# A block of weights fetched later in the prologue, and its two parts made between halves of h

## The chip, the cores and the metric

One core of a Trainium2 chip. The metric is device time in microseconds, the median of several runs. The engines are TensorE (PE), VectorE (DVE), ScalarE (ACT), GpSimd (POOL) and SyncE (SP), which issues every DMA of this kernel.

## What is computed

One step of a hybrid decoder layer over a prompt of 2048 rows and 8 sample rows, width 1024, in float32. Cut to what bears on this case:

```
mod = c @ w_ada + b_ada
shift, scale, gate = split(mod, 3)
h = rms_norm(x, norm_g) * (1 + scale) + shift
proj = h @ w_in      # q, k, v, za for window attention; q, f, i, z for the recurrence
... window attention with sinks; HGRN2 recurrence; both gated ...
y = sigmoid(h @ w_merge + b_merge) gates (ya @ w_proj_a) and (yb @ w_proj_b)
out = x + gate * (y @ w_out)
```

## The kernel before, in words

**Products in three parts.** Each operand of a dense product is split into a high part (float32r, made by ScalarE with a copy) and a low part (the rest, made by GpSimd with a subtraction). TensorE sums high x high, high x low and low x high (`dense`, lines 719 to 755).

**Tiles.** The prompt goes in four iterations of 512 rows. Each iteration is a list of units; a unit is one TensorE result in bank D0 or D1, run in two halves of the contraction (`hf_` 0 and 1), with side tasks between. The first four units of iteration 0 are B tiles: 128 rows of h against the three blocks q3, k and v. A block is 1024 x 128 weights, 512 KB. k and v are fetched in pieces of 128 numbers (512 bytes), q3 in pieces of 64, into one of three raw buffers (`block_dmas`, line 466). Block numbers 0, 1 and 2 are q3, k and v.

**The prologue.** mod needs all of `w_ada`'s first 2048 columns. They come in two halves, each as eight DMAs of 512 KB in pieces of 2 KB: `ada_load(k, 0)` (lines 523, 524), then `ada_load(k, 1)` (lines 633, 634). The last DMA of a half goes to the tile th_t. TensorE multiplies a half as pairs of tiles land (`ada_half`, line 678), turns the result rows into columns (`turn_rows`, line 688), and VectorE makes shift and scale from them (`modulation`, line 1239). The first half serves contraction slices 0 to 3 of h, the second slices 4 to 7. `modulate_half(t, q)` (line 1229) makes half q of tile t of h from the turned x, ScalarE its high part (`h_high_half`, line 982; semaphore `h_hi`), GpSimd its low part (lines 1701 to 1704; semaphore `h_lo`).

**Order on each engine, written out by hand.** SyncE: first-half modulation weights, blocks q3, k, v (lines 631, 632), second-half modulation weights, then small constants, then the gate weights. ScalarE: the high parts of the three blocks (lines 999, 1000), h halves (0,0) and (1,0), after the eighth modulation step (`p_mod` 8) the copy of a result bank (line 1003), h halves (0,1), (1,1), and those of tiles 2 and 3. GpSimd: the low parts of the three blocks (lines 1699, 1700), four subtractions each (`split_lo`, line 1677), then the eight low halves of h. TensorE: the first half of modulation, turns of x tiles 0 and 1, the second half of modulation, `turn_rows(1)`, dense half 0 of unit 0, the eight turns of x tile 2, dense half 1 of unit 0, the turns of x tile 3, and so on.

**What TensorE waits for.** Ahead of the first half of a unit, the low parts of all its blocks and with unit 0 the first low half of h:

```
s.wait_ge("w_lo", it * NB + blocks[-1] + 1)
...
if it == 0 and u < NT:
    s.wait_ge("h_lo", (1, 3, 2, 4, 5, 6, 7, 8)[2 * u + hf_])
```

For unit 0 the first of these is `w_lo` >= 3: the low parts of q3, k and v. Semaphores count up in the order in which the parts are made. SyncE issues block 3 only after the first side task that reads raw block 0 (line 808).

Of the kernel before, what the change touches and what calls it, by code (L numbers as in the profile page):

```python
# [50 lines left out]
NSLOT, NRAW = 6, 3  # L51
# [39 lines left out]
SPOT, HOLDER, ATTACH, BURST_AT = [], [], {}, {}  # L91
# [165 lines left out]
def h_tiles(it, t):  # L257

    return 8 + 4 * it + t + 1 if it >= 0 else 2 * t + 2
# [52 lines left out]
def build(nc, A, O):  # L312

    ctx = ExitStack()
    with ctx:
# [93 lines left out]
        def f32(ap):  # L409
            return ap.bitcast(F32)  # L410
# [55 lines left out]
        def block_dmas(n):  # L466

            kind, j = BLOCKS[n % NB]
            dst = w_raw[:, n % NRAW]
            if kind in ("q", "za"):  # L470
                c = (C_QA if kind == "q" else C_ZA) + DH * j
                return [(dst[:, :, DH * g:DH * g + DH],
                         w_in[:, c + 256 * g:c + 256 * g + DH].rearrange("(k p) c -> p k c", p=P))
                        for g in range(G)]
            if kind == "pa":
                cs = slice(P * j, P * j + P)
                return [(dst[DH * g:DH * g + DH, 0:4, :],
                         w_pa[256 * g:256 * g + 256, cs].rearrange("(m p) c -> p m c", p=DH))
                        for g in range(G)] + [(dst[:, 4:8, :],
                                               w_pb[:, cs].rearrange("(h p) c -> p h c", p=P))]  # L480
            base = {"f": C_FB, "qb": C_QB, "k": C_KA, "v": C_VA, "ib": C_IB, "zb": C_ZB}
            src, c0 = ((w_in, base[kind] + P * j) if kind in base else
                       (w_out, P * j) if kind == "out" else (w_merge, P * j + (D if kind == "gb" else 0)))
            return [(dst, src[:, c0:c0 + P].rearrange("(k p) c -> p k c", p=P))]
# [16 lines left out]
        def _(sp):  # L501
            s = Eng(sp, "none", S)

            def load(dst, src, name, **kw):
                s.done(sp.dma_start(dst, src, **kw), name, by=16)  # L505
# [6 lines left out]
            def ada_load(k, h):  # L512
                load(ada[k].rearrange("p (s h n) -> p s h n", s=2, h=2)[:, :, h],
                     A["w_ada"][0, P * k:P * k + P, 0:2 * D].rearrange("p (s h n) -> p s h n", s=2, h=2)[:, :, h], f"ada{KT * h + k}")
# [11 lines left out]
            def weights(n):  # L526
                if n >= NRAW:
                    s.wait_ge("w_lo", n - NRAW + 1)
                    if n - NRAW in bursts:
                        s.wait_ge(*bursts[n - NRAW])  # L530
                for dst, src in block_dmas(n):
                    load(dst, src, f"w_in{n % NRAW}")
# [95 lines left out]
                    s.freed(1, "sOT", 1)  # L628
                    load(O[1][:, 0, :], rowsS[:, 0:D], "fin")

            for n in range(NRAW):
                weights(n)
            for k in range(KT):
                ada_load(k, 1)
            load(ones[:, :], A["c_ones"], "p_load2")
            load(eye32[:, :], A["c_eye32"], "p_load2")
            load(lm_in, A["c_lmask"], "p_load2")
# [318 lines left out]
        def _(act):  # L956
# [3 lines left out]
            def split_hi(n):  # L960
                s.wait_ge(f"w_in{n % NRAW}", came[n])
                if HOLDER[n] >= 0:
                    s.unit_full(*divmod(HOLDER[n], NU))
                s.done(fn(w_hi[:, SLOT[n % NB]], w_raw[:, n % NRAW], ACT.Copy), "w_hi")  # L964
# [17 lines left out]
            def h_high_half(t, q):  # L982
                s.freed(-1, "xT", t) if q else s.wait_ge("hm", t + 1)
                k = slice(4 * q, 4 * q + 4)
                s.done(fn(h_hi[:, k, P * t:P * t + P], hf[t % 2][:, k], ACT.Copy), "h_hi")
# [10 lines left out]
                scale_x(-1, t, x_p[t])  # L996
            s.wait_ge("p_lb", 1)
            s.done(fn(lbt[:, 1:3, :], lbt[:, 1:3, :], ACT.Exp), "p_exp0")
            for n in ATTACH[-1]:
                split_hi(n)  # L1000
            h_high_half(0, 0), h_high_half(1, 0)
            s.wait_ge("p_mod", 8)
            s.done(fn(mod_rows[:, 512:1024], pb["D1"][:, :], ACT.Copy), "p_rows")
            h_high_half(0, 1), h_high_half(1, 1)
            for t in (2, 3):
                h_high_half(t, 0), h_high_half(t, 1)
# [665 lines left out]
        @blk.gpsimd  # L1672
        def _(pool):
            g_ = nc.gpsimd
            s = Eng(pool, "pool_step", S)

            def split_lo(n):
                s.wait_ge("w_hi", n + 1)
                c = SLOT[n % NB]
                for k in range(0, KT, 2):  # L1680
                    ins = g_.tensor_tensor(w_lo[:, c, k:k + 2], w_raw[:, n % NRAW, k:k + 2], f32(w_hi[:, c, k:k + 2]),  # L1681
                                           ALU.subtract)
                s.done(ins, "w_lo")

            def h_low(it, t):
                s.wait_ge("h_hi", h_tiles(it, t))
                c = slice(P * t, P * t + P)
                for k in range(0, KT, 2):
                    ins = g_.tensor_tensor(h_lo[:, k:k + 2, c], hf[t % 2][:, k:k + 2], f32(h_hi[:, k:k + 2, c]), ALU.subtract)
                s.done(ins, "h_lo")  # L1690

            def low(dst, hi, n):
                s.wait_ge("yh", n + 1)
                src = yf[:, n % 2, :]
                if dst.shape[-1] != TB:
                    src = src.rearrange("p (m n) -> p m n", m=4)
                s.done(g_.tensor_tensor(dst, src, f32(hi), ALU.subtract), "yl", n + 1)

            for n in ATTACH[-1]:
                split_lo(n)  # L1700
            for n, (t, q) in enumerate(((0, 0), (1, 0), (0, 1), (1, 1), (2, 0), (2, 1), (3, 0), (3, 1))):
                s.wait_ge("h_hi", n + 1)
                k, c = slice(4 * q, 4 * q + 4), slice(P * t, P * t + P)
                s.done(g_.tensor_tensor(h_lo[:, k, c], hf[t % 2][:, k], f32(h_hi[:, k, c]), ALU.subtract), "h_lo")
            for it in range(NIT):
                for u in range(NU):
                    for hf_ in (0, 1):
                        if hf_:
                            if UNITS[u] == ("pb", 7):
                                s.wait_ge("y7h", it + 1)  # L1710
                                s.done(g_.tensor_tensor(y_lo[:, 7, 0:P], yf[:, 1, 0:P], f32(y_hi[:, 7, 0:P]), ALU.subtract), "y7l")
                                s.wait_ge("yh", 16 * it + 16)
                                s.done(g_.tensor_tensor(y_lo[:, 7, P:TB], yf[:, 1, P:TB], f32(y_hi[:, 7, P:TB]),
                                                        ALU.subtract), "yl", 16 * it + 16)
                            for n in ATTACH.get(it * NU + u, []):
                                split_lo(n)
                        for task, a, _, key in SIDE.get((it, u, hf_), []):
                            if task == "at0":
                                if it:
                                    s.full(it - 1, "xT", 3)  # L1720
                                    s.freed(it - 1, "xT", 3)
                                else:
                                    s.freed(0, "gb", 0)
                                    s.freed(0, "gS", 0)
                                for c in range(0, 2048, 512):
                                    ins = g_.memset(R1[:, c:c + 512], 0.0)
                                s.done(ins, "at0")
                            elif task == "hh":
                                h_low(it, a)
                            elif task == "PV":  # L1730
                                c = slice(P * a, P * a + P)
                                low(ya_lo[:, :, c], ya_hi[:, :, c], 16 * it + a)
                            elif task == "yT":
                                c = slice(P * a, P * a + P)
                                low(yb_lo[:, :, c], yb_hi[:, :, c], 16 * it + 4 + a)
                            elif task == "vB":
                                s.wait_ge(f"s_st{a}", 16)
                                o = s_st[a].rearrange("p (h n) -> p h n", h=HB)
                                s.done(g_.tensor_tensor(o, o, fS[:, :, a:a + 1].broadcast_to([P, HB, P]), ALU.mult), "s_f")
                        if hf_ and UNITS[u][0] == "pb" and UNITS[u][1] < 7:  # L1740
                            j = UNITS[u][1]
                            low(y_lo[:, j, :], y_hi[:, j, :], 16 * it + 8 + j)
# [56 lines left out]
```

## Time and profile before

| | us |
|---|---|
| median of 3 runs | 1580.97 |
| lowest and highest run | 1580.01, 1585.47 |
| profiled execution | 1582.4 |
| its span in the trace | 1580.4 |

The profile shows one execution, with times in microseconds from the start of the span. "PEclk", or the third figure from the end in a stretch, is the clock that the throttle granted to TensorE as a share of full speed: 1 is 2.4 GHz, 0.5 is 1.2 GHz. The DMA share is the mean busy share of the core's 16 DMA engines; it can read slightly above 1. In brackets behind an instruction stands how long its engine was idle before it, and what released it. L750 and L753 are the dense matmuls, L685 the modulation matmuls, L692 the turns of the result rows, L964 a block's high part, L1681 a block's low part, L985 a high half of h, L1704 a low half of h.

### The profile page before, as it was taken

The numbers are of one execution on the slowest core, as the hardware profiler recorded it, in microseconds if no ns is written. First come the engines' busy times: TensorE is split into PE (matmuls) and PEld (weight loads), VectorE is DVE, ScalarE is ACT, GpSimd is POOL, SyncE is SP. The second block draws the span as 40 slices with busy tenths as digits, with TensorE's granted clock in tenths as the row PEclk, the third lists the DMA queues.
The fourth block names the chain that finished last, engine by engine and source line by source line (L and its number), as shares of the span: only waits on it lengthen the run. The fifth ranks groups of instructions, "written<-read, shape, count | busy, mean of one in ns | idle before, by whom it ended". The sixth has DMA issues, their size and how long they took to land.

```text
span 1580.4 us, 32835 instructions
## 1 busy us (share of the span) xinstructions
PE 1547.7 (98%) x13544; PEld 1257.3 (80%) x13544; DVE 776.6 (49%) x1946; ACT 554.8 (35%) x1131; POOL 824.6 (52%) x1080
## 2 busy tenths in 40 slices
PE   5999999999999999999999999999999999999998
PEld 2787788877888777888778877888888977788886
DVE  3667455233458865432345775722334775623132
ACT  4334323434322541433422352244432353243330
POOL 2435324457674552455756373437777363437671
PEclk9999999999999999999999999999999999999999
DMA  9723212344565331233365331224455331223351
GB/s 316 236 75 95 69 56 68 93 121 120 173 170 130 95 95 52 71 97 118 94 188 135 84 101 53 82 67 120 142 179 145 87 108 55 69 67 93 101 167 62
DMA packets 304972, 175.88 MB, mean 111 GB/s; under 512 B 74158, under 2 KB 290567, under 8 KB 304808
## 3 DMA queue, kind: packets, MB, share of 16 engines
q1 hardware_dynamic: 304824, 173.79, 37.8%
q8 instruction: 107, 1.75, 0.5%
q14 instruction: 41, 0.34, 0.1%
HBM read 159.69 MB, written 11.96 MB: 109 GB/s over the span
## 4 chain that ended last, share of the span: by engine, by line
PE 95%; DVE 2%; SPq 2%; DMA 1%; issue 1%; ACT 0%; DVEq 0%
PE ps_D L753 56%; PE ps_D L750 25%; PE ps_XD L808 2%; SPq L505 2%; PE ps_XA L907 1%; PE ps_XB L885 1%; PE ps_XB L933 1%; PE ps_XA L938 1%; PE ps_XB L932 1%; PE ps_XA L918 1%; DMA th_t<-in_w_ada 1%; PE ps_XA L885 1%; PE ps_XB L918 0%; PE ps_XC L925 0%; PE ps_XC L820 0%
## 5 line engine op out<-in xcount | busy, mean ns | idle before, releaser
L1681 POOL TENSOR_TENSOR w_lo_t<-w_raw,w_hi_t 128x256 fp32r<-128x256 f32 x928 | 678.3, 764 | 628.6 <-ACT w_hi_t L964 628.6
L753 PE MATMUL ps_D<-h_hi_t,w_hi_t 128*128 128x512 f32 x1024 | 412.9, 403 | 0.0
L753 PE MATMUL ps_D<-h_lo_t,w_hi_t 128*128 128x512 f32 x1024 | 399.9, 391 | 0.0
L753 PE MATMUL ps_D<-h_hi_t,w_lo_t 128*128 128x512 f32 x1024 | 399.9, 391 | 0.0
L964 ACT ACTIVATE w_hi_t<-w_raw 128x1024 fp32r<-128x1024 f32 x232 | 240.2, 1051 | 80.5 <-PE ps_D L750 44.7
L753 PEld LDWEIGHTS ps_D<-h_hi_t,w_hi_t 128*128 128x128 f32 x1024 | 192.3, 188 | 49.1 <-issue 12.0
L753 PEld LDWEIGHTS ps_D<-h_hi_t,w_lo_t 128*128 128x128 f32 x1024 | 192.2, 188 | 41.8
L753 PEld LDWEIGHTS ps_D<-h_lo_t,w_hi_t 128*128 128x128 f32 x1024 | 192.6, 188 | 36.1
L750 PE MATMUL ps_D<-w_hi_t,h_hi_t 128*128 128x384 f32 (+1 forms) x384 | 141.0, 367 | 2.2 <-issue 1.5
L750 PE MATMUL ps_D<-w_lo_t,h_hi_t 128*128 128x384 f32 (+1 forms) x384 | 136.3, 355 | 0.0
L750 PE MATMUL ps_D<-w_hi_t,h_lo_t 128*128 128x384 f32 (+1 forms) x384 | 136.0, 354 | 0.0
L750 PE MATMUL ps_D<-w_hi_t,y_hi_t 128*128 128x512 f32 x256 | 101.1, 395 | 0.0
L750 PE MATMUL ps_D<-w_lo_t,y_hi_t 128*128 128x512 f32 x256 | 99.7, 390 | 0.0
L750 PE MATMUL ps_D<-w_hi_t,y_lo_t 128*128 128x512 f32 x256 | 99.7, 390 | 0.0
L1355 DVE SCALAR_TENSOR_TENSOR acc_t<-th_t,ps_D 128x512 f32<-128x512 f32 x24 | 16.5, 688 | 139.3 <-PE ps_D L753 139.3
L1031 ACT ACTIVATE th_t<-ps_D,bm_half 128x512 f32<-128x512 f32 x48 | 33.1, 689 | 142.1 <-PE ps_D L753 142.1
L750 PEld LDWEIGHTS ps_D<-w_hi_t,h_hi_t 128*128 128x128 f32 x384 | 72.4, 189 | 10.0 <-issue 3.6
L1107 ACT ACTIVATE p_or_hf<-p_or_hf,sm 128x160 f32<-128x160 f32 x128 | 53.5, 418 | 72.5 <-DVE sm L1482 68.8
L750 PEld LDWEIGHTS ps_D<-w_hi_t,h_lo_t 128*128 128x128 f32 x384 | 72.5, 189 | 6.1 <-issue 1.4
L750 PEld LDWEIGHTS ps_D<-w_lo_t,h_hi_t 128*128 128x128 f32 x384 | 72.4, 188 | 5.3
L1435 DVE TENSOR_TENSOR qq<-qq,ff 128x1024 f32<-128x1024 f32 x28 | 40.9, 1460 | 70.4 <-PE ps_XB L885 44.8
L1524 DVE SCALAR_TENSOR_TENSOR state<-state,ff,ps_XA 128x128 f32<-128x128 f32 x64 | 18.0, 342 | 112.8 <-PE ps_XA L938 112.8
(391 smaller groups left out, 2375.7 us busy)
## 6 DMA issues: line engine op xcount, KB each, us to landing
w_raw<-in_w_in SPq DMA_DIRECT2D x72, 512.0 KB, 4.0
w_raw<-in_w_merge SPq DMA_DIRECT2D x64, 512.0 KB, 4.0
w_raw<-in_w_in SPq DMA_DIRECT2D x64, 256.0 KB, 4.0
w_raw<-in_w_out SPq DMA_DIRECT2D x32, 512.0 KB, 3.8
x_or_AT<-in_x_prompt SPq DMA_DIRECT2D x20, 512.0 KB, 5.1
w_raw<-in_w_proj_a SPq DMA_DIRECT2D x64, 128.0 KB, 3.0
w_raw<-in_w_proj_b SPq DMA_DIRECT2D x32, 256.0 KB, 3.2
xr<-in_x_prompt SPq DMA_DIRECT2D x16, 512.0 KB, 5.3
```

The costliest lines, as they stand in the source:

```text
L505: s.done(sp.dma_start(dst, src, **kw), name, by=16)
L750: ins = mm(bank[:, 0:P * nb].rearrange("p (n c) -> p n c", c=P), a[:, k, P * j:P * j + P], w[:, s0:s0 + nb, k, :], start=go, stop=end)
L753: ins = mm(bank[:, :], w[:, s0, k0 + k, :], a[:, k, :], start=go, stop=end)
L808: ins = mm(bank[32 * (k % 4):32 * (k % 4) + 32, P * c:P * c + P], hS[:, k, :], raw[:, k, :], start=k < 4, stop=k >= 4)
L885: ins = mm(bank[row:row + left, m * col:m * col + m], kk[:, h, c + 32 * g:c + 32 * g + left], right, start=True, stop=True)
L964: s.done(fn(w_hi[:, SLOT[n % NB]], w_raw[:, n % NRAW], ACT.Copy), "w_hi")
L1031: s.leave(fn(dst, bank[:, :], ACT.Tanh, scale=0.5, bias=bm_half[:, c:c + 1]), it, u)
L1107: fn(p_t[:, m, :], p_t[:, m, :], ACT.Exp, bias=negm[:, m:m + 1], accum_out=rsum[:, m:m + 1])
L1355: leave(stt(acc[:, :], thx("ga", j), 1.0, bank[:, :], ALU.add, ALU.mult), it, u)
L1435: s.done(tt(qr, qr, fl[:, :, :, 0:1].broadcast_to(shape), ALU.mult))
L1524: ins = stt(state[:, h, :], state[:, h, :], ff[:, h, P * a:P * a + 1], bank[:, P * h:P * h + P], ALU.mult, ALU.add)
L1681: ins = g_.tensor_tensor(w_lo[:, c, k:k + 2], w_raw[:, n % NRAW, k:k + 2], f32(w_hi[:, c, k:k + 2]), ALU.subtract)
```

## The change

The v block (number 2) is issued behind the second-half modulation weights. Its high part comes on ScalarE behind the copy of the result bank, its low part on GpSimd between the second and the third low half of h, after GpSimd's wait for the third high half. Nothing else is edited.

```diff
--- before.py
+++ after.py
@@ -628,10 +628,10 @@
                     s.freed(1, "sOT", 1)
                     load(O[1][:, 0, :], rowsS[:, 0:D], "fin")
 
-            for n in range(NRAW):
-                weights(n)
+            weights(0), weights(1)
             for k in range(KT):
                 ada_load(k, 1)
+            weights(2)
             load(ones[:, :], A["c_ones"], "p_load2")
             load(eye32[:, :], A["c_eye32"], "p_load2")
             load(lm_in, A["c_lmask"], "p_load2")
@@ -996,11 +996,11 @@
                 scale_x(-1, t, x_p[t])
             s.wait_ge("p_lb", 1)
             s.done(fn(lbt[:, 1:3, :], lbt[:, 1:3, :], ACT.Exp), "p_exp0")
-            for n in ATTACH[-1]:
-                split_hi(n)
+            split_hi(0), split_hi(1)
             h_high_half(0, 0), h_high_half(1, 0)
             s.wait_ge("p_mod", 8)
             s.done(fn(mod_rows[:, 512:1024], pb["D1"][:, :], ACT.Copy), "p_rows")
+            split_hi(2)
             h_high_half(0, 1), h_high_half(1, 1)
             for t in (2, 3):
                 h_high_half(t, 0), h_high_half(t, 1)
@@ -1696,11 +1696,12 @@
                     src = src.rearrange("p (m n) -> p m n", m=4)
                 s.done(g_.tensor_tensor(dst, src, f32(hi), ALU.subtract), "yl", n + 1)
 
-            for n in ATTACH[-1]:
-                split_lo(n)
+            split_lo(0), split_lo(1)
             for n, (t, q) in enumerate(((0, 0), (1, 0), (0, 1), (1, 1), (2, 0), (2, 1), (3, 0), (3, 1))):
                 s.wait_ge("h_hi", n + 1)
                 k, c = slice(4 * q, 4 * q + 4), slice(P * t, P * t + P)
+                if n == 2:
+                    split_lo(2)
                 s.done(g_.tensor_tensor(h_lo[:, k, c], hf[t % 2][:, k], f32(h_hi[:, k, c]), ALU.subtract), "h_lo")
             for it in range(NIT):
                 for u in range(NU):
```

## Rows read from the trace of the kernel before

**Rows 1.** The page: TensorE's busy time, and the chain that ended last by engine.
```profile
PE 1547.7 (98%) x13544; PEld 1257.3 (80%) x13544; DVE 776.6 (49%) x1946; ACT 554.8 (35%) x1131; POOL 824.6 (52%) x1080
...
PE 95%; DVE 2%; SPq 2%; DMA 1%; issue 1%; ACT 0%; DVEq 0%
```

**Rows 2.** Waits of TensorE, 44 to 200 us (total, times, longest us).
```profile
PE ps_XC L692 <- DVE qq L1292: 0.9, 1, 0.9
PE ps_D L750 <- DVE yf_t L1321: 0.7, 1, 0.7
```

**Rows 3.** Chain of waits, 0 to 80 us (start, length us, what).
```profile
28.95 12.91 DMA th_t<-in_w_ada
...
41.99 1.05 PE ps_D L685 x4
...
44.75 1.95 PE ps_XC L692 x16
46.71 3.21 PE ps_D L750 x12
...
51.38 2.08 PE ps_D L750 x12
```

**Rows 4.** Timeline of TensorE (start, length us, instruction, idle before it).
```profile
32.34 1.03 PE L685 MATMUL ps_D<-qq,cT_or_ab 128*32 128x512 f32 x1 [3.26 <-DMA ff<-in_w_ada]
...
46.56 0.42 PE L750 MATMUL ps_D<-w_hi_t,h_hi_t 128*128 128x384 f32 x1
...
48.11 0.52 PE L750 MATMUL ps_D<-w_hi_t,h_lo_t 128*128 128x384 f32 x1
48.43 0.52 PE L750 MATMUL ps_D<-w_lo_t,h_hi_t 128*128 128x384 f32 x1
...
49.71 1.67 PE L705 MATMUL ps_XA<-ident,s_st_lo 128*128 128x128 f32 x8
51.14 0.42 PE L750 MATMUL ps_D<-w_hi_t,h_hi_t 128*128 128x384 f32 x1
```

**Rows 5.** Timeline of GpSimd, 20 to 90 us.
```profile
25.95 8.25 POOL L1681 TENSOR_TENSOR w_lo_t<-w_raw,w_hi_t 128x256 fp32r<-128x256 f32 x12 [25.51 <-ACT w_hi_t L964]
...
49.42 2.69 POOL L1704 TENSOR_TENSOR h_lo_t<-p_or_hf,h_hi_t 128x512 fp32r<-128x512 f32 x2 [12.77 <-ACT h_hi_t L985]
...
61.74 5.57 POOL L1681 TENSOR_TENSOR w_lo_t<-w_raw,w_hi_t 128x256 fp32r<-128x256 f32 x8 [2.50 <-ACT w_hi_t L964]
...
83.25 3.34 POOL L1681 TENSOR_TENSOR w_lo_t<-w_raw,w_hi_t 128x256 fp32r<-128x256 f32 x4 [3.03 <-ACT w_hi_t L964]
```

**Rows 6.** Timeline of ScalarE, 20 to 60 us.
```profile
26.58 1.06 ACT L964 ACTIVATE w_hi_t<-w_raw 128x1024 fp32r<-128x1024 f32 x1 [0.70 <-DMA w_raw<-in_w_in]
28.68 1.06 ACT L964 ACTIVATE w_hi_t<-w_raw 128x1024 fp32r<-128x1024 f32 x1 [1.04 <-DMA w_raw<-in_w_in]
...
43.94 0.60 ACT L1003 ACTIVATE qq<-ps_D 128x512 f32<-128x512 f32 x1 [10.31 <-PE ps_XD L685]
48.71 0.63 ACT L985 ACTIVATE h_hi_t<-p_or_hf 128x512 fp32r<-128x512 f32 x1 [4.18 <-DVE p_or_hf L1235]
```

**Rows 7.** Stretches: busy us by engine, granted clock, DMA share, GB/s.
```profile
24.00:26.00 2.00, 2.00 (x16) 1.36 (x13) 1.18 (x2) 1.06 (x1) 0.04 (x1) 1.00 1.03 278
26.00:28.00 2.00, 2.00 (x22) 1.81 (x20) 0.11 (x1) 1.06 (x1) 2.00 (x3) 1.00 1.05 268
...
32.00:34.00 2.00, 1.66 (x4) 0.43 (x6) 0.96 (x4) 0.85 (x2) 2.00 (x4) 0.50 1.04 389
...
40.00:42.00 2.00, 0.01 (x2) 0.04 (x3) 0.00 (x0) 0.00 (x0) 0.00 (x0) 1.00 0.64 227
46.00:48.00 2.00, 2.00 (x14) 2.00 (x14) 1.19 (x6) 0.00 (x0) 0.00 (x0) 0.90 1.01 408
48.00:50.00 2.00, 2.00 (x8) 1.90 (x8) 1.96 (x7) 0.63 (x1) 0.58 (x1) 0.50 1.04 416
50.00:52.00 2.00, 2.00 (x13) 2.00 (x12) 1.22 (x5) 0.63 (x1) 1.87 (x2) 0.75 1.04 389
```

## The prediction

> **What bounds the kernel now.** I read the page first, to see which engine sets the time. TensorE is busy for 98% of the span and makes 95% of the chain that ended last [rows 1]. Then the list of TensorE's waits after the prologue: from 44 to 200 us it waits twice, for 0.9 and 0.7 us [rows 2]. The reader is to see that nothing after the prologue has room to take up a delay: what the start of the first dense unit gains or loses should reach the end.
>
> Then the chain of waits over the prologue. The last second-half modulation weights (th_t) are issued at 28.95 and hold the chain for 12.91 us, until TensorE takes them at 41.99. The last matmuls on it follow, the copy to mod_rows, the 16 row turns from 44.75 to 46.70, and at 46.71 the dense matmuls [rows 3]. The one idle time between is the 0.9 us for the copy [rows 2]. So today the first dense half starts when TensorE has done its own work, not when a weight is ready. TensorE's timeline gives 46.56 for its first matmul [rows 4]. The v block is not on that path: its low part is the last third of a GpSimd stretch that ends at 25.95 + 8.25 = 34.20 [rows 5], 12.4 us before that matmul.
>
> **The change part by part.**
>
> **1. The transfer of v leaves the queue ahead of the second modulation half.** SyncE issues one DMA fewer there and one more behind; the work of issuing is the same. The price of v in the queue: ScalarE waits for each block's data and starts on k at 26.58 and on v at 28.68, so v took 2.10 us [rows 6]. In 24 to 28 us the engines moved 278 and 268 GB/s at full share [rows 7]; 512 KB, which is 524,288 bytes, by 270 is 1.94 us. I take 1.9. Lower bound: while modulation weights of the same size moved, the rate was 389 GB/s [rows 7], so 1.35 us. Upper bound: near th_t's landing (40 to 42 us) the engines were busy for a share of only 0.64 [rows 7], so the last piece sits on an engine that lags; if v's pieces cost that engine more by the unused 0.36 of 2 us, v is worth 2.1 + 0.7 = 2.8. Gain 1.9 (1.35 to 2.8).
>
> The Trainium skill (DMA: Bandwidth & Descriptors, Specifications) says that pieces of 512 bytes or more move at line rate. v is fetched in pieces of 128 numbers, 512 bytes, and this trace disagrees: its blocks move at 268 to 278 GB/s where modulation weights get 389. By the page the gain would be 1.35 and the result 0.55 us later than my sum.
>
> **2. ScalarE's high part of v moves behind the copy of the second half's rows.** The copy starts at 43.94 and the next instruction, the high part of h's tile 0, second half, only at 48.71, after 4.18 us idle for VectorE [rows 6]. The 1.06 us of v fit there. v's data: as many bytes lie ahead of it as now lie ahead of th_t, so it lands near 41.9 (where th_t lands now), before ScalarE asks at about 44.54 - 1.9 = 42.6. Cost 0. If that cover were gone, it would need v to land after 45.7.
>
> **3. GpSimd's low part of v moves, and behind a wait.** This decides. In the new code GpSimd first waits for the third high half of h, and only then runs the four subtractions for v. The third high half is ScalarE's at 48.71, with 0.63 us, so it ends at 49.34; GpSimd answers at 49.42 [rows 5]. TensorE's first dense half waits for the low part of all three blocks, v's included. Today that wait was met at 34.2. In the new order it is met when four subtractions after 49.42 are done. Their price: 12 took 8.25 us, so 2.75 for four; the next eight took 5.57, so 2.79 [rows 5]. I take 2.8, with bounds 2.75 and 3.34, the dearest group [rows 5]. With 0.05 for the handover, the first dense matmul comes at 49.42 + 2.80 + 0.05 = 52.27 by today's clock of events, where it now comes at 46.56: 5.7 us later. Both times shift together by the 1.9 of part 1, since the third high half hangs on VectorE's modulation (the releaser of the instruction at 48.71 [rows 6]), and that on th_t.
>
> Who waits behind it: on GpSimd the low parts of h, third and fourth half, come 2.8 us later, at about 52.3 and 53.5 less 1.9. TensorE asks for the third only after the first dense half and eight turns, 4.6 us after its new start (as from 46.56 to 51.14 [rows 4]), about 55. VectorE's tile 2 waits for that third half as well, but also for TensorE's turns, which end later. Cost of both 0; the cover is TensorE's own delay. TensorE holds everything behind its wait, above all the turns of tile 2, which stand behind the dense half in its order and can't fill the gap. All later loads hang on TensorE (the next weight block is issued once the first sample burst is done) and shift with it.
>
> **4. The clock.** TensorE will stand idle from the end of the row turns (46.70 - 1.9 = 44.8) to 50.4, for 5.6 us. Before, it stood idle for 3.26 us ahead of 32.34 [rows 4], and the granted clock then fell to 0.50 (1.2 GHz), where it still was in 32 to 34 us with TensorE busy [rows 7]. The first dense half also meets the low clock today: 0.32 us from one matmul to the next at 48.11 [rows 4], against 2.08 / 12 = 0.17 in the second half [rows 3]; in 46 to 52 us with mean clocks of 0.90, 0.50 and 0.75 [rows 7]. Between levels of 1 and 0.5 those means stand for 0.4 + 2.0 + 1.0 = 3.4 us at the low one. After the longer gap I expect the whole first half at 1.2 GHz, 12 x 0.32 = 3.84 against 46.56 to 49.71 = 3.15 now: 0.7 more. Bounds: 0 (the low stretch has the same length), and 1.7 (it is twice as long, 3.4 us more at half rate).
>
> **5. What is free.** SyncE issues ones, eye32, the mask, the rope table and the gains behind v as before. The gate weights wait for the modulation matmuls, which come no later than now; their first user stands in unit 3.
>
> **The sum.** -1.9 + 5.7 + 0.7 = +4.5 us. The profiled execution took 1582.4 us (span 1580.4), which makes 1586.9; it is 1.4 above the median shown, 1580.97, and from the median the forecast is 1585.5.
>
> **Rivals.**
>
> A, **the low clock lasts.** After 5.6 us idle TensorE works at 1.2 GHz not for one dense half but through turns, bursts and unit 1. For it: the gap is longer than the 3.26 us that brought the low clock before, and the second gap, for th_t, may bring it for the last eight modulation matmuls too. Against: once TensorE was busy from 46.56, the clock was back within 50 to 52 us [rows 7]. Each us at 1.2 GHz costs 0.5. From 11.6 us of low clock on (3.4 now and 2 x (7.9 - 3.8) more) the kernel is slower by over 0.5%; with 14 us the sum is -1.9 + 5.7 + 5.3 = +9.1, 1590.1. The Trainium skill (TensorE: Matmul & The Clock Gate, What's actually happening) has the low clock as the default that activity lifts; by it the gap has a price of its own, which agrees with the falls at both gaps here. Chance 0.12.
>
> B, **the transfer isn't what th_t waits for** (the change doesn't do what it says). If the lagging engine sets th_t's landing whatever v does, part 1 gives 0: 5.7 + 0.7 = +6.4, 1587.4. For: the share of 0.64 at the end [rows 7]. Against: full shares from 24 to 28 and from 32 to 34 us [rows 7]. Chance 0.10.
>
> C, **the delay is taken up later**, and only the earlier modulation is left: a stretch bound by VectorE could absorb it. For: TensorE's 0.7 us wait for yf_t [rows 2] is VectorE's. Against: VectorE's tiles there come from TensorE's own units, so they shift too. Then -1.9, 1579.1. Chance 0.05.
>
> **How the numbers follow.** Forecast 0.70; A 0.12, B 0.10, C 0.05, anything else 0.03. The likeliest case alone spans +2.9 (gain 2.8, clock 0) to +6.6 (gain 1.35, GpSimd 0.54 dearer, clock 1.7): 1583.9 to 1587.6. For the 8 in 10 I add about 2 us on each side, because three runs of one kernel lay between 1580.01 and 1585.47: 1582 to 1590, which leaves out C and half of A. 0.5% is 7.9 us, about what a measurement here can tell from no change. Beyond +7.9 lie half of A (0.06), a third of B (0.03) and scatter (0.06): slower 0.15. Faster by 7.9 has no mechanism: 0.02. Same 0.83.
>
> **What would show it.** In the new profile: TensorE takes th_t near 40.1; the third high half of h ends near 47.4; four subtractions for v from 47.5 to 50.3, ahead of the low part of h's third half; TensorE idle about 5.6 us, released by GpSimd's w_lo; first dense matmul near 50.4. Wrong if the dense half starts before 48 or after 53, if th_t lands at 41.8 still (B), if the clock is at 0.5 beyond 56 us (A), or if the end comes no later although the first dense matmul does (C).

## The result and the profile after

The changed kernel takes 1585.35 us (median of 20 runs, 1583.57 to 1589.21); the kernel before takes 1580.35 beside it (20 runs). The ratio is 1.0031, interval 1.0025 to 1.0037: 5.0 us slower. The profiled execution took 1585.01, with a span of 1583.1.

The page again has TensorE at 98%; its share of the chain fell by a point to VectorE (against [rows 1]):

```profile
PE 1548.7 (98%) x13544; PEld 1258.6 (80%) x13544; DVE 780.4 (49%) x1946; ACT 554.9 (35%) x1131; POOL 824.6 (52%) x1080
...
PE 94%; DVE 3%; SPq 2%; DMA 1%; issue 1%; ACT 0%; POOL 0%; DVEq 0%
```

The waits of TensorE after the prologue, 44 to 200 us, against [rows 2]. The 0.9 us for the copy has left this stretch, because it now ends before 44; a wait of 5.5 us for v's low part is new; the later one, 0.7 us for yf_t, is unchanged:

```profile
PE ps_D L750 <- POOL w_lo_t L1681: 5.5, 1, 5.5
...
```

The chain of waits through the prologue, against [rows 3] (start, length us, what):

```profile
27.20 11.09 DMA th_t<-in_w_ada
...
41.19 1.97 PE ps_XC L692 x16
...
43.74 1.37 DVE p_or_hf L1235 x4
45.14 0.64 ACT h_hi_t L985
...
45.84 2.78 POOL w_lo_t L1681 x4
...
48.66 4.21 PE ps_D L750 x12
```

Before, the row turns handed over to the dense half directly. Now VectorE's modulation, ScalarE's third high half and the four subtractions on GpSimd stand between. TensorE's timeline, against [rows 4]:

```profile
38.42 0.59 PE L685 MATMUL ps_D<-s_st_hi,cT_or_ab 128*32 128x512 f32 x1 [1.35 <-DMA th_t<-in_w_ada]
...
48.66 0.69 PE L750 MATMUL ps_D<-w_hi_t,h_hi_t 128*128 128x384 f32 x1 [5.53 <-POOL w_lo_t L1681]
49.15 0.52 PE L750 MATMUL ps_D<-w_hi_t,h_lo_t 128*128 128x384 f32 x1
...
52.67 1.65 PE L705 MATMUL ps_XA<-ident,s_st_lo 128*128 128x128 f32 x8
54.08 0.43 PE L750 MATMUL ps_D<-w_hi_t,h_hi_t 128*128 128x384 f32 x1
```

GpSimd and ScalarE, against [rows 5, 6]. GpSimd sits idle for 11.52 us until the third high half, and only then makes v's low part; ScalarE had started on v's high part at 40.86, and still waited 3.23 us for VectorE afterwards:

```profile
25.33 5.51 POOL L1681 TENSOR_TENSOR w_lo_t<-w_raw,w_hi_t 128x256 fp32r<-128x256 f32 x8 [24.89 <-ACT w_hi_t L964]
...
45.84 2.77 POOL L1681 TENSOR_TENSOR w_lo_t<-w_raw,w_hi_t 128x256 fp32r<-128x256 f32 x4 [11.52 <-ACT h_hi_t L985]
```

```profile
40.37 0.60 ACT L1002 ACTIVATE qq<-ps_D 128x512 f32<-128x512 f32 x1 [7.38 <-PE ps_XD L685]
40.86 1.05 ACT L964 ACTIVATE w_hi_t<-w_raw 128x1024 fp32r<-128x1024 f32 x1
45.14 0.63 ACT L985 ACTIVATE h_hi_t<-p_or_hf 128x512 fp32r<-128x512 f32 x1 [3.23 <-DVE p_or_hf L1235]
```

Stretches, against [rows 7] (the last three figures are granted clock, DMA share, GB/s). The clock lies at 0.50 from before 44 until about 54. Its mean of 0.92 in 42 to 44 us puts the fall at about 43.7, some 0.6 us after the gap begins (48.66 - 5.53 = 43.13):

```profile
42.00:44.00 2.00, 1.14 (x11) 1.05 (x10) 0.75 (x4) 0.00 (x0) 0.00 (x0) 0.92 0.76 305
44.00:46.00 2.00, 0.00 (x0) 0.00 (x0) 1.96 (x7) 0.63 (x1) 0.16 (x1) 0.50 1.02 418
...
52.00:54.00 2.00, 2.00 (x10) 1.91 (x10) 0.00 (x0) 0.00 (x0) 0.00 (x0) 0.52 1.04 387
54.00:56.00 2.00, 2.00 (x14) 2.00 (x13) 1.54 (x5) 0.18 (x1) 0.00 (x0) 1.00 0.26 101
56.00:58.00 2.00, 2.00 (x39) 1.80 (x41) 1.80 (x6) 1.08 (x2) 1.35 (x2) 1.00 0.00 0
```

SyncE's issues of the constant `ones`, which stands behind the weights, and of the first gate weights (ff). First the kernel before, then the changed kernel:

```profile
30.38 1.23 SPq L505 DMA_DIRECT2D ones<-in_c_ones  x1
37.35 0.43 SPq L505 DMA_DIRECT2D ff<-in_w_ada  x1
```

```profile
28.86 4.92 SPq L505 DMA_DIRECT2D ones<-in_c_ones  x1
38.53 0.43 SPq L505 DMA_DIRECT2D ff<-in_w_ada  x1
```

### The profile page after: what moved, and what is told of

Same layout as the page of the kernel before. It is cut to its first block, busy times and chain, and to the rows that moved or that the text cites. A ratio compares the mean times of both kernels' runs of the same rounds, so it can differ in the third digit from the quotient of the medians.

```text
span 1583.1 us, 32836 instructions
## 1 busy us (share of the span) xinstructions
PE 1548.7 (98%) x13544; PEld 1258.6 (80%) x13544; DVE 780.4 (49%) x1946; ACT 554.9 (35%) x1131; POOL 824.6 (52%) x1080
## 3 DMA queue, kind: packets, MB, share of 16 engines
HBM read 159.69 MB, written 11.96 MB: 108 GB/s over the span
## 4 chain that ended last, share of the span: by engine, by line
PE 94%; DVE 3%; SPq 2%; DMA 1%; issue 1%; ACT 0%; POOL 0%; DVEq 0%
PE ps_D L753 55%; PE ps_D L750 25%; PE ps_XD L808 2%; SPq L505 2%; PE ps_XA L907 1%; PE ps_XB L885 1%; PE ps_XB L933 1%; PE ps_XA L938 1%; PE ps_XB L932 1%; PE ps_XA L918 1%; PE ps_XA L885 1%; DMA th_t<-in_w_ada 1%; PE ps_XB L918 0%; PE ps_XC L925 0%; PE ps_XC L820 0%
## 5 line engine op out<-in xcount | busy, mean ns | idle before, releaser
L1435 DVE TENSOR_TENSOR qq<-qq,ff 128x1024 f32<-128x1024 f32 x28 | 40.9, 1462 | 69.7 <-PE ps_XB L885 44.5
```

Of the source, the lines that this page charges most:

```text
L1435: s.done(tt(qr, qr, fl[:, :, :, 0:1].broadcast_to(shape), ALU.mult))
```

## The experiments

All medians stand against runs of the kernel before on the same chip. In each trace three events place the prologue: TensorE takes th_t, the first dense half starts, the second dense half starts. In e8 TensorE was still busy with extra matmuls when th_t landed, so its th_t says less of the landing. e2 and e12 are the same kernel, and so are e4 and e10.

| kernel | ratio, interval | th_t | first half | second half | span |
|---|---|---|---|---|---|
| before | | 41.99 | 46.56 | 51.14 | 1580.4 |
| before, again | | 39.66 | 44.23 | 48.78 | 1577.9 |
| changed | 1.0031, 1.0025 to 1.0037 | 38.42 | 48.66 | 54.08 | 1583.1 |
| e1 low part before the wait | 1.0006, 0.9997 to 1.0015 | 38.43 | 44.81 | 50.38 | 1579.8 |
| e2 order only | 1.0043, 1.0031 to 1.0056 | 40.22 | 50.47 | 55.17 | 1584.4 |
| e12 order only, again | 1.0037, 1.0023 to 1.0051 | 40.46 | 50.70 | 56.27 | 1585.0 |
| e3 queue only | 1.0011, 1.0002 to 1.0020 | 38.63 | 45.91 | 51.35 | 1581.0 |
| e4 low part on VectorE | 1.0000, 0.9992 to 1.0009 | 39.20 | 44.01 | 48.55 | 1578.3 |
| e10 the same, again | 1.0000, 0.9991 to 1.0010 | 39.27 | 44.07 | 48.01 | 1580.5 |
| e6 and high part first | 1.0000, 0.9991 to 1.0010 | 38.75 | 44.32 | 49.87 | 1578.6 |
| e9 k and v behind | 1.0002, 0.9993 to 1.0011 | 37.70 | 45.08 | 50.65 | 1580.6 |
| e7 low part one step later | 1.0036, 1.0024 to 1.0049 | 40.01 | 51.47 | 56.72 | 1586.5 |
| e5 gap filled | 1.0049, 1.0036 to 1.0061 | 39.05 | 51.01 | 54.30 | 1587.7 |
| e8 idle times filled | 1.0013, 1.0005 to 1.0022 | 40.38 | 45.75 | 49.92 | 1581.4 |

**e1: the low part of v ahead of GpSimd's wait.**

```diff
+                if n == 2:
+                    split_lo(2)
                 s.wait_ge("h_hi", n + 1)
                 k, c = slice(4 * q, 4 * q + 4), slice(P * t, P * t + P)
-                if n == 2:
-                    split_lo(2)
```

> The changed kernel, with GpSimd's low part of v one line earlier, ahead of its wait for the third high half of h. Theory (the wait costs the time, the transfer gains): the low part starts when ScalarE's high part of v ends, about 3.5 us after TensorE takes th_t, so the first dense matmul comes 6.35 us after th_t is taken, against 4.6 in the kernel before and 10.2 in the changed one. Against the kernel before: th_t's gain (1.9 to 3.6 us) less 1.8: 0 to -1.8 us, ratio 0.999 to 1.000. Rival (the loss comes from the transfer's new place, not from the wait): the time stays at the changed kernel's, about +5 us, ratio 1.003.

Measured: 1581.74 against 1580.49, ratio 1.0006. One line's place in GpSimd's order is worth most of the loss: TensorE's wait falls from 5.53 to 1.67 us, and the first dense half starts 6.38 us after th_t, as expected. The rival falls. But the time did not come below the kernel before. The theory had left out the clock: the dense half still ran at 1.2 GHz.

```profile
38.43 0.59 PE L685 MATMUL ps_D<-s_st_hi,cT_or_ab 128*32 128x512 f32 x1 [1.55 <-DMA th_t<-in_w_ada]
...
44.81 0.69 PE L750 MATMUL ps_D<-w_hi_t,h_hi_t 128*128 128x384 f32 x1 [1.67 <-POOL w_lo_t L1681]
...
48.82 1.80 PE L705 MATMUL ps_XA<-ident,s_st_lo 128*128 128x128 f32 x8
50.38 0.42 PE L750 MATMUL ps_D<-w_hi_t,h_hi_t 128*128 128x384 f32 x1
```

From 44.81 to 48.82 the dense half takes 4.01 us, where it takes 3.15 at [rows 4]: 0.86 more. With the transfer's gain of 1.4 (below) the sum is -1.4 + 1.8 + 0.86 = +1.3, and +1.0 (by the ratio) to +1.3 (by the medians) was measured.

**e2 and e12: the new order on the engines, the old queue.** Edit against the changed kernel:

```diff
-            weights(0), weights(1)
+            for n in range(NRAW):
+                weights(n)
             for k in range(KT):
                 ada_load(k, 1)
-            weights(2)
```

> The new order on ScalarE and GpSimd with the old order of the DMA queue (v ahead of the second modulation half). Theory: the whole loss without the gain, 5.7 for the wait and 0.9 for the clock, about +6.6 us or more, ratio 1.004. The difference to the changed kernel's +5.0 is what the transfer's place is worth at the median: 1.9 by my sum (then +6.9), 3.6 by the changed kernel's one profile (then +8.6). Rival (th_t's landing does not hang on v): the same +5.0 as the changed kernel.

> The new order on the engines with the old queue order, once more, for the median and another landing of th_t. Theory: +6.6 to +6.9 us again, ratio 1.0043, th_t taken near 40.5. Rival (the transfer's place is worth nothing at the median): +5.0.

Measured: 1586.45 against 1580.49 and 1586.87 against 1580.17, so +6.0 and +6.7. This is the loss without the gain, and it shows that the queue's new place is worth something: 1.0 to 1.7 us of medians (1.0 to 1.9 by the ratios 1.0037, 1.0043 and 1.0031). The intervals overlap, so its size is known only roughly. The rival of no gain is the less likely, not excluded by these medians alone. The wait is the same 5.53 us:

```profile
40.22 0.59 PE L685 MATMUL ps_D<-s_st_hi,cT_or_ab 128*32 128x512 f32 x1 [1.43 <-DMA th_t<-in_w_ada]
...
50.47 0.69 PE L750 MATMUL ps_D<-w_hi_t,h_hi_t 128*128 128x384 f32 x1 [5.53 <-POOL w_lo_t L1681]
```

**e11: the kernel before, profiled again.**

> The kernel before, profiled once more, for another reading of when TensorE takes th_t with v ahead of it in the queue (so far 41.99 here and 40.22 in the kernel with the new order alone; 38.4 to 40.0 with v behind). Theory (the first profile of the kernel before was a late one): near 40.5, first dense matmul near 45.1, span near 1579. Rival (42 is the usual landing): 41.5 to 42.5 and a span near 1580.4.

Measured in one run: 1579.85, span 1577.9. TensorE takes th_t at 39.66, not 41.99; from there on all is as before (4.57 us to the first dense matmul in both).

```profile
39.66 0.59 PE L685 MATMUL ps_D<-s_st_hi,cT_or_ab 128*32 128x512 f32 x1 [0.80 <-DMA th_t<-in_w_ada]
...
44.23 0.42 PE L750 MATMUL ps_D<-w_hi_t,h_hi_t 128*128 128x384 f32 x1
```

The four readings with v ahead are 41.99, 40.22, 39.66 and 40.46. The eight with v alone behind and nothing else in that wait are 38.42, 38.43, 38.63, 39.20, 39.27, 39.05, 38.75 and 40.01. The medians are 40.3 and 38.9: 1.4 us. The two groups overlap and come from several chips, so this too is a rough figure (the means differ by 1.6). Two single profiles, 41.99 and 38.42, would have said 3.6.

**e3: the new queue order alone**, with the high and low parts of all three blocks ahead of the halves of h as before.

```diff
-            for n in range(NRAW):
-                weights(n)
+            weights(0), weights(1)
             for k in range(KT):
                 ada_load(k, 1)
+            weights(2)
```

> The new order of the DMA queue with the old order on ScalarE and GpSimd (high part of v ahead of the first high halves of h, low part ahead of the low halves). Theory: th_t is taken 1.9 to 3.6 us earlier; ScalarE now waits for v's data and the copy behind it comes late, the first low half of h comes behind v's low part; the first dense matmul about 6.8 us after th_t, so -1.4 to +0.3 us against the kernel before, ratio 0.999 to 1.000. Rival (v lands late, well after 42 us): ScalarE holds everything, +2 us or more.

Measured: 1582.58, ratio 1.0011, so +1.7 to +2.1 us: more than the theory's range, and about what the rival had. But v did not land well after 42, as the rival had it: it was there at 40.64. ScalarE waits for v, and the copy and the turns stand behind it:

```profile
40.64 1.06 ACT L964 ACTIVATE w_hi_t<-w_raw 128x1024 fp32r<-128x1024 f32 x1 [12.73 <-DMA w_raw<-in_w_in]
...
42.64 0.58 ACT L1003 ACTIVATE qq<-ps_D 128x512 f32<-128x512 f32 x1
```

The copy of mod_rows comes at 42.64, 4.0 us after th_t is taken, against 2.0 in the changed kernel. Here too a dense half of 3.97 us at the low clock adds to the loss. The first dense matmul came 7.28 us after th_t, 0.5 later than expected.

**e4 and e10: v's low part on VectorE.** GpSimd's `split_lo(2)` is dropped, and VectorE gets:

```diff
             s.done(cp(mod_rows[:, 1536:2048], XD[:, :]), "p_rows")
+            s.wait_ge("w_hi", 3)
+            s.done(tt(w_lo[:, 2], w_raw[:, 2], f32(w_hi[:, 2]), ALU.subtract), "w_lo")
             modulation(1)
```

> The changed kernel, with v's low part made by VectorE in one subtraction behind its copy to mod_rows, where it now stands idle for 2.04 us. Theory: VectorE takes about 1.5 us for it (128x1024, as its other subtractions of that size), ends about 5.0 us after TensorE takes th_t, so the row turns hide nearly all and the gap is gone, with it the long low clock: th_t's gain less 0.5, -1.4 to -3.1 us against the kernel before, ratio 0.998 to 0.999. Rival (another wait takes the place of the removed one): no faster than the kernel before.

> The kernel with v alone behind and its low part on VectorE once more, beside the one with k and v behind. Theory: as before within 0.1% of the kernel before, with TensorE waiting 0.3 us at the first sample burst of the next weight blocks. Rival: its first time was a chance of the chip, and it is faster by 1 us or more.

Measured: ratio 1.0000 both times (medians 1580.24 against 1580.49, and 1581.88 against 1580.66). The gap is gone: VectorE's subtraction took 1.23 us and the dense half started 4.8 us after th_t. Yet no gain over the kernel before is seen; the intervals of 0.09% would hide one of up to 1.4 us. In the first profile th_t was followed by the second dense half after 9.35 us, against 9.15 in the kernel before, and the whole took what the second profile of the kernel before took (1578.3 and 1577.9). The second profile shows what can take back an earlier start. There the dense half ran at 2.4 GHz throughout and ended at 46.28, earlier than in any other kernel, and TensorE then met two waits that the kernel before does not have:

```profile
PE ps_XD L808 <- ACT srow L1071: 1.7, 1, 1.7
...
PE ps_D L750 <- POOL h_lo_t L1705: 0.7, 1, 0.7
```

The first hangs on the next weight block. It was issued at 51.94, behind the four gate-weight loads of 1 MB each, while the queue was full:

```profile
51.94 0.38 SPq L505
52.37 7.39 DMA w_raw<-in_w_in
59.78 1.06 ACT w_hi_t L964
```

```profile
52.00:54.00 2.00, 2.00 (x22) 1.82 (x11) 1.96 (x7) 0.63 (x1) 1.44 (x2) 1.00 1.05 395
...
56.00:58.00 2.00, 2.00 (x13) 1.91 (x12) 1.87 (x9) 0.00 (x0) 0.14 (x1) 1.00 0.77 143
```

In the changed kernel the queue is empty at 56 to 58 us (0 GB/s, above) and the same block is issued at 57.99. So in e10 part of the earlier start is given back near 60 us, to a queue that still carries gate weights. Behind the wait of 1.7 us the granted clock also fell, to a mean of 0.66 in 62 to 64 us and 0.50 in 64 to 66, where both profiles of the kernel before have 1.00. From the second dense half to the end e10 took 1532.5 us, against 1529.8 in e4 and 1529.1 to 1529.3 in the kernel before.

The gate weights come later by the change itself. In the nine profiles with v alone behind, SyncE is held at the issue of `ones` for 4.85 to 5.53 us, and the first gate load is issued at 38.5 to 39.9. In the four with v ahead the issue of `ones` takes 1.16 to 1.23 us, and the first gate load is issued at 35.2 to 37.4. Why that issue takes longer stays open.

**e6: also the high part ahead of ScalarE's wait for the eighth modulation step.**

```diff
+            split_hi(2)
             s.wait_ge("p_mod", 8)
             s.done(fn(mod_rows[:, 512:1024], pb["D1"][:, :], ACT.Copy), "p_rows")
-            split_hi(2)
```

> As the kernel with v's low part on VectorE, with ScalarE's high part of v ahead of its wait for the eighth modulation step, so that it runs when v's data lands (near 40) and not behind the copy. Theory: high part done 0.5 to 1 us earlier, VectorE's subtraction wholly under the row turns, first dense matmul 4.6 us after th_t instead of 4.8, and modulation of the next halves not late: 0.2 to 0.4 us less than that kernel, -0.2 to -0.6 us against the kernel before. Rival (v lands later than th_t by enough to hold the copy): 0.5 us or more slower than that kernel, since the copy and the turns wait.

Measured: 1581.10, ratio 1.0000; no gain over e4, by the medians a loss of 0.9 us, as the rival had it. ScalarE waited for v until 40.32, 1.57 us after th_t was taken; the copy of mod_rows slipped behind it, and TensorE's idle time ahead of the turns grew from 0.85 to 1.25 us.

```profile
41.91 2.56 PE L692 MATMUL ps_XC<-misc,qq 128*128 128x9 f32 x16 [1.25 <-ACT qq L1003]
44.32 0.67 PE L750 MATMUL ps_D<-w_hi_t,h_hi_t 128*128 128x384 f32 x1
```

**e9: k and v behind**, high parts of both behind the copy, k's low part on GpSimd ahead of its wait, v's on VectorE.

```diff
-            weights(0), weights(1)
+            weights(0)
             for k in range(KT):
                 ada_load(k, 1)
-            weights(2)
+            weights(1), weights(2)
...
-            split_hi(2)
+            split_hi(1), split_hi(2)
...
-            split_lo(0), split_lo(1)
+            split_lo(0)
...
+                if n == 2:
+                    split_lo(1)
                 s.wait_ge("h_hi", n + 1)
```

> Both k and v behind the second modulation half; high parts of both on ScalarE behind its copy, k's low part on GpSimd ahead of its wait for the third high half of h, v's low part on VectorE behind its copy. Theory (th_t's landing goes by the bytes ahead of it): th_t is taken another 1.8 us earlier, near 36.6; the first dense matmul waits for v, which lands near 40, and for k's low part, and comes near 42.7, 1.3 us earlier than with v alone behind: -1 to -2 us against the kernel before, ratio 0.999. Rival (the work of two blocks behind their landing takes back what the earlier th_t gives): no faster than the kernel before.

Measured: 1581.03, ratio 1.0002. th_t is taken at 37.70 in its one profile, about 1.2 us earlier than the median with v alone behind, not 1.8. The work on two blocks takes it back. The two subtractions also ran at the same time and slowed each other, GpSimd's four to 3.76 us from 2.77 and VectorE's to 1.60 from 1.23:

```profile
41.27 3.76 POOL L1683 TENSOR_TENSOR w_lo_t<-w_raw,w_hi_t 128x256 fp32r<-128x256 f32 x4 [7.02 <-ACT w_hi_t L964]
```

```profile
42.17 1.60 DVE L1294 TENSOR_TENSOR w_lo_t<-w_raw,w_hi_t 128x1024 fp32r<-128x1024 f32 x1 [1.76 <-ACT w_hi_t L964]
```

The Trainium skill (SBUF — State Buffer, SBUF: two separate sides) says that VectorE with two SBUF inputs and a GpSimd instruction that reads SBUF take a shared port in turn; both rows fit that, but no run here tells it from another cause.

**e7: the low part of v one step later**, behind the third low half of h.

```diff
-                if n == 2:
-                    split_lo(2)
                 s.done(g_.tensor_tensor(h_lo[:, k, c], hf[t % 2][:, k], f32(h_hi[:, k, c]), ALU.subtract), "h_lo")
+                if n == 2:
+                    split_lo(2)
```

> The changed kernel, with the low part of v one step later still, behind the third low half of h (1.3 us of GpSimd). Theory (nothing later takes up a delay of the first dense half): 1.3 us more than the changed kernel, +6.3 us against the kernel before, ratio 1.004, and a TensorE wait of 6.8 us. Rival (part of such a delay is taken up in the stretches bound by VectorE): less than 0.5 us more.

Measured: 1586.27, ratio 1.0036, 0.9 us of median above the changed kernel, not 1.3. The wait grew by 1.22 us, to 6.75. By the profile nothing took the delay up (1529.8 us from the second dense half to the end, 1529.0 in the changed kernel), but the intervals of the two ratios overlap, so the medians alone don't decide.

**e5: the gap filled with matmuls.** Behind `turn_rows(1)`:

```diff
+            for _ in range(7):
+                mm(pb["D1"][:, :], ident[:, :], mod_rows[:, 0:512], start=True, stop=True)
```

> The changed kernel, with seven extra matmuls (128x512, into bank D1, which nobody reads then) on TensorE between the row turns and the first dense half; each takes about 0.45 us at 2.4 GHz and 0.9 at 1.2, so they fill 3 to 6 of the 5.5 us of the gap and delay nothing much. Theory (the gap's price has a part from the clock): with TensorE busy, the first dense half runs wholly or partly at 0.17 us per matmul instead of 0.32, 0.8 to 1.9 us less than the changed kernel, so +3.1 to +4.2 us against the kernel before, ratio 1.002 to 1.0027. Rival (the dense half is slow for another reason, its operands for one): same as the changed kernel, +5.0, with 0.32 us per matmul.

Measured: 1588.97, ratio 1.0049: slower than the changed kernel, against the theory's number. Each matmul ran as two instructions; the 14 took 7.81 us, more than the gap. The trace still answers the question that was asked. With TensorE busy ahead of it, the dense half ran at 0.17 us per matmul. The low clock came all the same (means of 0.60 and 0.55 in 44 to 48 us), but it met the extra matmuls and was over at 48:

```profile
43.63 7.95 PE L719 MATMUL ps_D<-qq,ident 128*128 128x512 f32 x14
51.01 0.74 PE L752 MATMUL ps_D<-w_hi_t,h_hi_t 128*128 128x384 f32 x1
51.59 0.34 PE L752 MATMUL ps_D<-w_hi_t,h_lo_t 128*128 128x384 f32 x1
...
53.51 1.04 PE L705 MATMUL ps_XA<-ident,s_st_lo 128*128 128x128 f32 x8
54.30 0.43 PE L752 MATMUL ps_D<-w_hi_t,h_hi_t 128*128 128x384 f32 x1
```

From 51.01 to 53.51 it takes 2.50 us with its first instruction, against 4.01. Although it starts 11.96 us after th_t (10.24 in the changed kernel), the second half starts after 15.25 (15.66). The clock is the cause of the slow dense half, and its operands are not. The loss came later: from the second half to the end 1533.4 us passed, where the kernels without extra matmuls need 1528.7 to 1530.0 (e10 with its late block 1532.5). Part of it is waits that have no releaser:

```profile
PE ps_XA L887 <- issue: 2.1, 2, 1.9
...
PE ps_XB L887 <- issue: 1.5, 3, 1.0
```

**e8: the idle times filled**, with three such matmuls ahead of the last pair of modulation weights and two behind `ada_half(1)`, on top of e6.

```diff
                 for p in range(4):
+                    if (h, p) == (1, 3):
+                        s.wait_ge("hm", 2)
+                        for _ in range(3):
+                            mm(pb["D0"][:, :], ident[:, :], mod_rows[:, 0:512], start=True, stop=True)
...
             ada_half(1)
+            for _ in range(2):
+                mm(pb["D0"][:, :], ident[:, :], mod_rows[:, 0:512], start=True, stop=True)
```

> As the kernel with high part first and low part on VectorE, with five extra matmuls in TensorE's idle times: three while it waits for th_t and two while it waits for the copy to mod_rows. Theory (the first dense half is slow because TensorE did little before it): if that work is enough to keep the clock at 2.4 GHz, the first dense half takes 2.1 us instead of 3.2 to 4.0, 1 to 1.7 us less than that kernel. Rival (the row turns ahead of the dense half count as rest, whatever comes before them): the clock falls all the same, no gain, and 0.2 to 0.5 us of loss for the two extra matmuls.

Measured: 1583.44, ratio 1.0013, 2.3 us of median slower than e6. The clock was low from about 29 to 36 us as in other kernels, but not after that: the dense half runs from 45.75 to 47.92, 2.17 us. That is what the theory asked for, but one profile does not show that the extra matmuls did it. e10 has no extra matmuls, and its dense half took 2.21 us at 2.4 GHz, while e4, the same kernel as e10, was at the low clock from about 44.5.

```profile
45.75 0.42 PE L756 MATMUL ps_D<-w_hi_t,h_hi_t 128*128 128x384 f32 x1
...
47.92 1.09 PE L709 MATMUL ps_XA<-ident,s_st_lo 128*128 128x128 f32 x8
49.92 0.44 PE L756 MATMUL ps_D<-w_hi_t,h_hi_t 128*128 128x384 f32 x1 [0.91 <-POOL h_lo_t L1711]
```

The time was lost around it. The three matmuls (2.84 us) ran to about 40.4, 0.9 us past th_t's landing, the two others delayed the turns, and TensorE then waited 0.91 us for the low part of h. From the second half to the end it took 1531.5 us, 1.5 to 2.8 more than the kernels without extra matmuls other than e10. The shorter dense half was worth less than the rest cost.

No version beat the kernel before; e1, e4, e6 and e9 can't be told from it.

## Why the prediction was right

**The sum.** Forecast +4.5, measured +5.0, inside the range given and below the 7.9 us that would have counted as slower. The times named as signs came earlier than forecast: th_t taken at 38.42 (forecast 40.1), the first dense matmul at 48.66 (50.4), close to the 48 that would have counted against the theory. The whole difference is in the landing of th_t, which was late in the one profile that the forecast started from (41.99, against 39.66 in e11). So the parts are better told from th_t. From th_t to the first dense half: 4.57 before, 10.24 after, so 5.67 (forecast 5.7). Its length: 3.15 before, 4.01 after, so 0.86 (forecast 0.7). Less the transfer, 1.4: +5.1.

**Part 1, the transfer: probably sized too large.** I took 1.9, with bounds of 1.35 and 2.8; the runs show 1.0 to 1.7 by medians, 1.0 to 1.9 by the ratios, and 1.4 by landings. The lower end, 1.35, worked out from 389 GB/s for modulation weights, lies nearer to most of these. The Trainium skill (DMA: Bandwidth & Descriptors, Specifications) has pieces of 512 bytes or more at line rate. The rate in the queue does not agree with it, 268 to 278 GB/s while these blocks passed [rows 7]; the 1.4 us by landings is near the 1.35 that the prediction worked out by it.

**Part 2, ScalarE: right.** v was issued at 27.71 and took 12.3 us to land, so about 40.0; ScalarE asked at 40.86 and did not wait. The margin was 0.9 us.

**Part 3, the wait on GpSimd: right.** Forecast wait 5.6, measured 5.53; subtractions 2.77 (taken at 2.8), begun at 45.84, 0.07 us behind the end of ScalarE's third high half. e1 shows that the wait for the third high half is the cause, and not v's transfer.

**Part 4, the clock: right in size, not shown in its reason.** The whole first half ran at 1.2 GHz, as forecast, and the turns behind it in part too, as before. But I put this down to the longer gap. In the changed kernel the clock fell some 0.6 us after the gap began (0.9 and 2.5 us after it in e12 and e2); e1, with a gap of 1.67 us, fell at the same point (about 43.8) and also had its whole first half at the low clock, and so had e3 and e6, with no gap right ahead of it (TensorE had waited 2.73 and 1.25 us ahead of the row turns). In the kernel before the low clock covers 3.4 us of this stretch [rows 7], from about 47.6, in e11 from about 45.0, in e10 it does not come at all. When it falls thus varies between executions of one kernel, and what the long gap added is not told apart from that. That the forecast of 0.7 met 0.86 is in part luck: a dense half that is wholly at the low clock can't lose more.

**Part 5: right in its result, wrong in its reason.** The gate weights cost nothing here, since the dense units start late. But their issue did not go by the modulation matmuls alone: the first was issued at 38.53 (before 37.35, in e11 35.56), behind an issue of `ones` that held SyncE for 4.92 us. I had taken the work of issuing as the same. From 40 to 42 us the changed kernel's queue moved 35 GB/s, against 227 before [rows 7]. e10 shows that late gate weights can bound an earlier start.

**The rivals.** A: the clock was back at 54 us, at the end of one dense half and its turns, not after unit 1. B: e2 and e12 against the changed kernel, and the landings, speak against it. C: the changed kernel passes the whole delay on (1529.0 us from the second half to the end, 1529.3 before).

## What to carry to other kernels

A step that is moved takes on the waits that stand ahead of it in its new place: read the wait above it, follow it back to its releaser, and ask which engine then waits for the step. Here a transfer worth about 1.4 us was bought with 5.7, although the place just above the wait was free. Ask also what now stands behind the moved transfer in the queue: here the gate weights came later by it. Size an effect of one or two microseconds from several profiles, since one landing in the prologue varied by 2.3 us between executions of the same kernel.

## What the runs showed that I had not expected

The landing of th_t in the kernel before was 41.99 in one execution and 39.66 in another, with the same work ahead of it.

Extra matmuls in an idle time of TensorE were not free. In neither kernel did they quite fit, and both kernels also took longer from the second dense half on. In e5 the waits without a releaser at the turns (L887) add up to 3.6 us after 80 us, where the kernel before has 0.5 at that line (L885 there), and the remainder of the kernel took 4.4 us longer. The cause is open; no run tells it apart.

The clock: with TensorE busy from 43.63 on, the low clock had passed by 51 us and the dense half met none of it; in e8 it did not come after 36 us, and in e10, without extra matmuls, it did not come before 62, while in e4, the same kernel, it came twice. So no run here shows that extra matmuls keep it away.
